# One GpSimd subtraction of 1024 columns per chunk of weights in place of two of 512

## What is computed

```python
h = rms_norm(x, norm_mix_g); proj = h @ w_in
gates = sigmoid(h @ w_gate); merged = sum(gates * up); x = x + merged @ w_out
a, g = split(rms_norm(x, norm_ffn_g) @ w_ffn_in, 2)
x = x + (silu(a) * g) @ w_ffn_out
```

## Time and profile before

| | |
|---|---|
| Median of three runs | 3445.1 us |
| The profiled execution's own time | 3441.26 us |
| Its span (first to last instruction) | 3439.4 us |
| TensorE (PE) busy | 3222.5 us, 94% |
| GpSimd (POOL) busy | 1974.3 us, 57% |
| VectorE (DVE) busy | 1401.9 us, 41% |
| ScalarE (ACT) busy | 745.3 us, 22% |
| Mean granted TensorE clock | 0.96 of full speed |

### The profile page before, as it was taken

How to read it: one execution, slowest core, us unless ns; L and a number is a source line. 1 busy time by engine, 2 the same in 40 slices (tenths; PEclk the granted TensorE clock), 3 DMA queues, 4 the chain that set the end, 5 groups by cost and what they waited for, 6 DMA issues and landing times.

```text
span 3439.4 us, 44451 instructions
## 1 busy us (share of the span) xinstructions
PE 3222.5 (94%) x14188; PEld 2516.5 (73%) x14188; DVE 1401.9 (41%) x2310; ACT 745.3 (22%) x1516; POOL 1974.3 (57%) x1528
## 2 busy tenths in 40 slices
PE   5898999999979889999999879989999999999998
PEld 3654887888756468788887656868888777878886
DVE  5545225221355352353425545452214544452223
ACT  3421102100234211120102335241002333230001
POOL 5234666776743266677767131847768433747765
PEclk8897999999989899999999889999999999999999
DMA  4111223222221122222222010322223111312222
GB/s 151 37 50 56 98 93 106 94 98 98 92 92 45 35 87 93 100 87 97 98 98 100 28 68 13 118 69 98 97 94 110 62 50 50 110 64 97 98 98 86
DMA packets 78347, 284.97 MB, mean 83 GB/s; under 512 B 8688, under 2 KB 9200, under 8 KB 77424
## 3 DMA queue, kind: packets, MB, share of 16 engines
q1 hardware_dynamic: 74736, 269.41, 23.1%
q10 hardware_dynamic: 3456, 13.50, 1.1%
HBM read 280.78 MB, written 2.10 MB: 82 GB/s over the span
## 4 chain that ended last, share of the span: by engine, by line
PE 78%; DVE 9%; ACT 3%; issue 1%; DVEq 0%; DMA 0%; ACTq 0%
PE pd L512 35%; PE pa L512 34%; PE pd L656 3%; PE po L675 3%; PE pa L664 1%; DVE b_lo L180 1%; DVE work L180 1%; DVE work L184 1%; ACT work L176 1%; DVE h_lo L188 1%; PE pd L575 1%; DVE pair L180 1%; DVE t L188 1%; PE pd L693 1%; PE po L707 1%
## 5 line engine op out<-in xcount | busy, mean ns | idle before, releaser
L465 POOL TENSOR_SCALAR w_hi<-w_raw 128x1024 fp32r<-128x1024 f32 x508 | 550.2, 1083 | 1392.9 <-PE pa L512 884.4
L512 PE MATMUL pa<-h_hi,w_hi 128*128 128x512 f32 x1888 | 754.1, 399 | 24.7 <-DVE h_lo L188 16.9
L469 POOL TENSOR_TENSOR w_lo<-w_raw,w_hi 128x512 fp32r<-128x512 f32 x508 | 743.5, 1464 | 0.0
L512 PE MATMUL pa<-h_lo,w_hi 128*128 128x512 f32 x1888 | 739.5, 392 | 0.0
L512 PE MATMUL pa<-h_hi,w_lo 128*128 128x512 f32 x1888 | 739.3, 392 | 0.0
L467 POOL TENSOR_TENSOR w_lo<-w_raw,w_hi 128x512 fp32r<-128x512 f32 x508 | 703.2, 1384 | 42.3
L512 PE MATMUL pd<-b_hi,w_hi 128*128 128x512 f32 x1152 | 456.8, 397 | 24.4 <-DVE b_lo L180 21.1
L512 PE MATMUL pd<-b_lo,w_hi 128*128 128x512 f32 x1152 | 452.4, 393 | 0.0
L512 PEld LDWEIGHTS pa<-h_hi,w_hi 128*128 128x128 f32 x1888 | 357.3, 189 | 129.8 <-issue 52.8
L512 PE MATMUL pd<-b_hi,w_lo 128*128 128x512 f32 x1152 | 451.7, 392 | 0.0
L512 PEld LDWEIGHTS pa<-h_lo,w_hi 128*128 128x128 f32 x1888 | 357.8, 190 | 75.9 <-issue 3.6
(11 more groups left out here) (154 smaller groups left out, 3417.9 us busy)
## 6 DMA issues: line engine op xcount, KB each, us to landing
w_raw<-in_w SPq DMA_DIRECT2D x508, 512.0 KB, 3.2
mrg<-in_mem ACTq DMA_DIRECT2D x4, 1024.0 KB, 4.8
mrg<-in_nabias ACTq DMA_DIRECT2D x2, 2048.0 KB, 8.7
x_res<-in_x SPq DMA_DIRECT2D x8, 256.0 KB, 5.7
out_y<-mrg ACTq DMA_DIRECT2D x8, 256.0 KB, 2.1
mrg<-in_count ACTq DMA_DIRECT2D x2, 512.0 KB, 3.9
kbuf<-in_delta ACTq DMA_DIRECT2D x2, 448.0 KB, 7.9
rope<-in_rope SPq DMA_DIRECT2D x1, 512.0 KB, 11.8
```

The costliest lines, as they stand in the source:

```text
L465: nc.gpsimd.tensor_scalar(w_hi[:, j], raw[:, j % RR], 1.0, 1.0, ALU.mult, ALU.mult).then_inc(rounded, 1)
L469: nc.gpsimd.tensor_tensor(w_lo[:, j, 512:1024], raw[:, j % RR, 512:1024], w_hi[:, j, 512:1024].bitcast(F32), ALU.subtract).then_inc(wsplit, 1)
L512: ins = mm(out, a, b, start=(first and k == 0 and e == 0), stop=(last and k == k_n - 1 and e == 2))
```

## The change

The two subtractions of 512 columns become one of 1024. What is read, computed and written is the same, as are the waits and the semaphore that is given at the end.

```diff
                 pool.wait_ge(rounded, i * RW + j + 1)
-                nc.gpsimd.tensor_tensor(w_lo[:, j, 0:512], raw[:, j % RR, 0:512], w_hi[:, j, 0:512].bitcast(F32),
-                                        ALU.subtract)
-                nc.gpsimd.tensor_tensor(w_lo[:, j, 512:1024], raw[:, j % RR, 512:1024],
-                                        w_hi[:, j, 512:1024].bitcast(F32), ALU.subtract).then_inc(wsplit, 1)
+                nc.gpsimd.tensor_tensor(w_lo[:, j], raw[:, j % RR], w_hi[:, j].bitcast(F32), ALU.subtract)\
+                    .then_inc(wsplit, 1)
```

## The result

The changed kernel has a median of 3488.77 us over four runs (3487.94 to 3489.99), the kernel before 3444.55 over its four. The ratio is 1.013, with a 95% interval of 1.0112 to 1.0147: slower by 44 us. The forecast was 3460 us with a range that ended at 3474. The direction was right, the size was not: the time rose by almost three times the 15 us forecast.

What follows compares the result with a forecast made beforehand. TensorE, busy 94% of the span, was taken to bound the kernel. Terms of 3.6 + 3.6 + 1.2 + 4.8 + 3.0 - 1.0 = 15.2 us, beside the 3445.1 us median, gave 3460 us; range 3446 to 3474.

Steps and rivals of the forecast that it cites:

- item 2: Last `h_lo` before a norm, six times in a first half, 0.6 us of slack: 6 x (1.2 - 0.6) = 3.6 us.
- Item 1: Last `b_lo` of the last group in three of four feed-forwards, no slack: 3 x 1.2 = 3.6 us longer.
- Item 3: Wait ahead of the first addition to the residual, at 925.01, in a first half: 1.2 us longer.
- The start that is saved: One GpSimd instruction start fewer per chunk, 508 in all, taken as 0.1 us each; GpSimd's idle time covers the saving.
- the inventory: VectorE's instructions on the chain longer than the shortest of their form, costed where they lay: 15.2 us in all.
- item 5: Twenty chunks with VectorE waits in both halves, 0.3 us each, halved: 20 x 0.3 / 2 = 3.0 us.
- item 4: Eight lone first-half waits in norms of heads and softmax, half counted: 8 x 1.2 / 2 = 4.8 us.
- The statement that TensorE never waits for GpSimd: GpSimd works ahead of TensorE, stopped by the ring; TensorE waits for VectorE instead, and GpSimd would still never be waited for.
- Absorbed: Rival: longer waits mostly fall where VectorE has time to spare; 4 us slower, 3449 us; chance 0.25.
- faster: Rival: the long subtraction lets VectorE in at its middle, so waits do not grow; 3433 us; chance 0.04.
- Piled up: Rival: all lone and paired waits count and the norms have no slack; 26.6 us slower, 3472 us; chance 0.17.
- the prediction's own sign: Forecast wrong if `h_lo` has no length above 1.9 us, or TensorE's idle time is not longer by 10 to 20 us.

Runs made afterwards that it cites:

- the tail alone: One subtraction of 1024 columns for chunks 32 to 507, two of 512 for chunks 0 to 31, against the kernel before: 3474.96 us, ratio 1.0081.

## Why the prediction was wrong, and where it was right

**The mechanism was right.** Long VectorE instructions end 0.5 us after GpSimd's, also with 1024 columns. The last tile of the first output projection in the changed kernel, beside the earlier trace rows:

```profile
600.07 2.40 POOL L467 TENSOR_TENSOR w_lo<-w_raw,w_hi 128x1024 fp32r<-128x1024 f32 x1
...
600.31 2.71 DVE L188 SCALAR_TENSOR_TENSOR h_lo<-x_res,par,h_hi 128x512 fp32r<-128x512 f32 x1 [0.85 <-ACT h_hi L176]
...
603.15 0.69 DVE L180 TENSOR_TENSOR qs<-po,pair 128x512 f32<-128x512 f32 x1
...
603.89 1.12 PE L559 MATMUL pa<-qs,mats 128*128 128x512 f32 x2 [0.40 <-DVE qs L180]
```

`h_lo` takes 2.71 us (1.61 before), `qs` ends at 603.84, and the norm's matmul starts at 603.89 after an idle 0.40 us; set against the kernel before, TensorE falls back 0.53 us at this point, where the forecast's item 2 had 0.6. The other five norm ends are 0.5 to 0.7. Two rows on which that part rests are not in the groups that it names: `h_lo` alone, and the first VectorE wait of the pair (rows 10 has ScalarE's at that time). They are, in the kernel before:

```profile
936.55 0.75 DVE L188 SCALAR_TENSOR_TENSOR h_lo<-x_res,par,h_hi 128x512 fp32r<-128x512 f32 x1 [0.85 <-ACT h_hi L176]
...
962.02 1.40 DVE L188 SCALAR_TENSOR_TENSOR t<-mrg,par,rope 128x256 f32<-128x256 f32 x1
```

**Item 1 was right.** The end of the second feed-forward's last group, beside the earlier trace rows:

```profile
1860.71 2.70 POOL L467 TENSOR_TENSOR w_lo<-w_raw,w_hi 128x1024 fp32r<-128x1024 f32 x1
...
1861.86 2.10 DVE L180 TENSOR_TENSOR b_lo<-t,b_hi 128x512 fp32r<-128x512 f32 x1 [0.70 <-ACT b_hi L176]
...
1864.02 0.50 PE L510 MATMUL pd<-b_hi,w_hi 128*128 128x512 f32 x1 [1.25 <-DVE b_lo L180]
```

`b_lo` takes 2.10 us instead of 1.01, and TensorE's idle time goes from 0.15 to 1.25 us: 1.1 us, and so in all three. **Item 3 was right**: at the place of the earlier trace rows TensorE loses 1.1 us, though 0.5 of it is made good 26 us later, where its idle time before a norm's chunk falls from 0.85 to 0.32 us. The start that is saved was 0.14 us (2.40 us alone, against 2.54 for two halves that begin 1.25 us apart) and was taken as 0.1.

**The step that failed first is the inventory, by its reach.** I took VectorE's long instructions "on the chain" and read the chain as if it covered the span. The shares of the engines on it were 78, 9, 3 and 1%, 91% in all: the missing 9% were the warning. The chain of the kernel before in order of time (start, length, what, how many) begins, but for 0.19 us of issue, with this piece, 302.56 us into the span (the 313.6 us of an expectation above are not in that view):

```profile
302.56 22.02 PE pa L512 x96
```

There was no term for the 300 us in front of it, where the norms, the first attention and the first pooling lie. The experiment with the long chunks at the head alone puts 9 us there (5 to 13). At the very start of the changed kernel two waits follow one another:

```profile
24.67 2.38 DVE L188 SCALAR_TENSOR_TENSOR rope<-pair,rope 128x256 f32<-128x256 f32 x1
...
28.02 2.92 DVE L188 SCALAR_TENSOR_TENSOR h_lo<-x_res,par,h_hi 128x512 fp32r<-128x512 f32 x1 [0.31 <-ACT h_hi L176]
28.03 2.35 POOL L467 TENSOR_TENSOR w_lo<-w_raw,w_hi 128x1024 fp32r<-128x1024 f32 x1
```

**The second is item 5, 0.3 us for a chunk with both waits.** It supposed that GpSimd's work for the chunk is over after the pair. In the second pooling another chunk follows at once, and the stretch cost 5.5 us (3.5 with its own chunks alone made long) where item 5 gives its eight chunks 8 x 0.3 / 2 = 1.2 us. The first pooling lies in the missing 300 us.

**The third is that a stage in which VectorE is the bound was not seen.** The two cross attentions with their projections cost 12.8 us, 9.0 of it idle. The forecast saw that its chain passed through VectorE there, but had no row for VectorE's own pace per tile (3.2 us) beside TensorE's (2.7 us), and so it halved (item 4) what is hardly covered there: the one wait ahead of `x_res` takes TensorE's idle time from 0.75 to 2.34 us, by 1.6 us. The `h_lo` behind it is the one of the earlier trace rows. In the kernel before it met a rounding and took 1.57 us; in the changed kernel, with everything shifted, it meets a whole subtraction and takes 2.95 us. The inventory left each wait where it lay in the kernel before, and so it had no longer wait here.

**The fourth is TensorE's busy time, held constant.** It rose by 14.4 us in the traces. Behind the 2.34 us of idle time above the clock was lower in the changed kernel, but not in every kernel with that wait. How much of the 14.4 us is the change stays open, since between 70 and 260 us the same matmuls took 6.1 us more in an execution without any change there, and 7.2 us more between 970 and 1215 us in that of the kernel with eight long chunks.

**The statement that TensorE never waits for GpSimd held.** The list above puts two weight loads, ahead of the two output projections of the first block, down to `w_lo`, 10.7 us in all. The timeline of the first of them:

```profile
548.95 2.89 POOL L467 TENSOR_TENSOR w_lo<-w_raw,w_hi 128x1024 fp32r<-128x1024 f32 x1
...
552.50 0.28 PEld L510 LDWEIGHTS pd<-b_hi,w_hi 128*128 128x128 f32 x1 [5.31 <-POOL w_lo L467]
552.53 0.76 PE L510 MATMUL pd<-b_hi,w_hi 128*128 128x512 f32 x1 [4.92 <-DVE b_lo L180]
```

`w_lo` is over at 551.84, while the first `b_lo`, which had to wait for it, ends at 552.39 by the single rows, just ahead of the matmul; the second place is the same. TensorE had stood there for `b_lo` in the kernel before too, for 3.97 and 4.05 us, and stands 0.95 and 0.93 us longer.

**The rivals.** "Absorbed" fell with the result and with the kernel without subtraction, "faster" with the rows of the changed kernel above: `h_lo` isn't let in half way. "Piled up" had the right direction, and its 26.6 us lie near what the tail alone measured (28 us, 19 to 37). That is in part luck: in that kernel's trace the second pooling and the two cross attentions with their projections make 14 of 36 us, and these are the stages that steps two and three above had wrong. Head and tail together are 37 of the 44 us, which agree within their intervals. By the prediction's own sign it was wrong too: `h_lo` had lengths above 1.9 us, and TensorE's idle time was longer by 33 us, not by 10 to 20.

## What to carry to other kernels

Where two engines exclude each other, cost a longer instruction by what the exclusion already costs: leave the work out once, and scale with the square of the length. That held here for longer pieces (128 + 896, and the whole); cutting finer gave back less than the squares say, 8 us instead of 21, so it is no safe measure of the price. Before taking an inventory from a chain, add up its shares and look at where it begins. And ask of each stage which engine sets its pace; where it is the one that is made to wait, a longer wait has little to hide behind.

## What the runs showed of the hardware

In the second pooling, where VectorE and GpSimd both had instructions queued, they alternated by single instructions, so that the number of instructions into which one's work was cut set how fast the other moved: three turns a chunk instead of two took 5.5 us of loss to 1.7. A VectorE instruction that had waited ended 0.54 to 0.55 us after the GpSimd instruction, whether that had 512 columns or 1024 (602.47 and 603.02 us in the changed kernel). And a subtraction of 128 columns lasts 0.51 us on the mean beside the 0.82 us of one of 256, so cutting each half in four (eight pieces) raised GpSimd's work by about 1.2 us a chunk (3.93 to 5.15) without stopping TensorE for more than 13.6 us in all.
